# Feed-forward products of a streaming encoder step in two passes, one for each half of the frames

## The reference

```
for layer in range(2):
    x = rms_norm(h, g[0])
    m = mixer_ab(x) if layer == 0 else pool_mixer(x)
    h = h + rms_norm(m, g[1])
    x = rms_norm(h, g[2])
    gu = x @ ffn_w_in[layer]                               # 1024 x 5632
    y = (silu(gu[..., :2816]) * gu[..., 2816:]) @ ffn_w_out[layer]
    h = h + rms_norm(y, g[3])
```

## Time and profile before

| | us |
|---|---|
| median of 3 runs | 1102.53 |
| lowest, highest | 1100.94, 1103.25 |
| the profiled execution | 1102.74 |
| its span, first to last instruction | 1100.7 |
| PE busy in the span | 1063.5 |
| DVE busy | 506.5 |
| ACT busy | 363.5 |
| POOL busy | 43.7 |

### The profile page before, as it was taken

One profiled execution on the slowest core, in us unless ns is written; L12 is line 12 of the kernel. 1 busy time (PEld: TensorE's weight loads), 2 busy tenths in 40 slices (PEclk: granted clock), 3 DMA queues, 4 the chain that ended last, 5 costly groups with the idle time before them and its releaser, 6 DMA issues.

```text
span 1100.7 us, 19933 instructions
## 1 busy us (share of the span) xinstructions
PE 1063.5 (97%) x8219; PEld 1033.6 (94%) x8219; DVE 506.5 (46%) x813; ACT 363.5 (33%) x598; POOL 43.7 (4%) x48
## 2 busy tenths in 40 slices
PE   6999989989999999999999899899999999999997
PEld 4799789989999999999999799899999999999995
DVE  4386743855344444432222669544444443422225
ACT  5422344542222222222222665422222222222222
POOL 0070120000000000000000011000000000000000
PEclk9999999999999999999999999999999999999997
DMA  6422112213322332323323210232232232233212
GB/s 222 96 63 81 40 39 77 58 55 99 95 76 86 94 87 76 91 79 93 91 79 104 66 44 20 66 107 76 86 94 86 76 95 86 79 92 93 76 53 82
DMA packets 166532, 89.69 MB, mean 81 GB/s; under 512 B 11976, under 2 KB 163647, under 8 KB 166492
## 3 DMA queue, kind: packets, MB, share of 16 engines
q1 hardware_dynamic: 164620, 86.99, 27.0%
q10 hardware_dynamic: 1648, 1.78, 0.5%
q0 software_dynamic: 224, 0.35, 0.1%
HBM read 86.53 MB, written 2.58 MB: 81 GB/s over the span
## 4 chain that ended last, share of the span: by engine, by line
PE 85%; DVE 9%; ACT 2%; issue 2%; DMA 1%; SPq 0%; ACTq 0%; DVEq 0%
PE ps L453 27%; PE ps L454 27%; PE ps L455 27%; DVE h L1577 2%; DVE tmp L1547 1%; PE ps L518 1%; DVE acc_pre L1563 1%; DVE xlo L1551 1%; DVE wlo L1310 1%; DMA x_tok<-in_x_sample_dram 1%; PE ps L861 1%; ACT whi L936 0%; PE ps L471 0%; DVE va L1369 0%; PE ps L502 0%
## 5 line engine op out<-in xcount | busy, mean ns | idle before, releaser
L453 PE MATMUL ps<-xhi,whi 128*128 128x256 f32 (+1 forms) x1600 | 467.3, 292 | 13.7 <-DVE xlo L1551 5.8
L454 PE MATMUL ps<-xlo,whi 128*128 128x256 f32 (+1 forms) x1600 | 463.2, 289 | 0.0
L455 PE MATMUL ps<-xhi,wlo 128*128 128x256 f32 (+1 forms) x1600 | 462.0, 289 | 0.0
L453 PEld LDWEIGHTS ps<-xhi,whi 128*128 128x128 f32 x1600 | 304.3, 190 | 18.3 <-DVE xlo L1551 8.5
L1310 DVE TENSOR_TENSOR wlo<-raw,whi 128x1024 fp32r<-128x1024 f32 (+2 forms) x175 | 196.3, 1122 | 270.3 <-ACT whi L936 266.1
L455 PEld LDWEIGHTS ps<-xhi,wlo 128*128 128x128 f32 x1600 | 304.8, 190 | 0.0
L454 PEld LDWEIGHTS ps<-xlo,whi 128*128 128x128 f32 x1600 | 304.7, 190 | 0.0
L936 ACT ACTIVATE whi<-raw 128x1024 fp32r<-128x1024 f32 (+2 forms) x176 | 167.9, 954 | 197.3 <-PE ps L455 174.0
L455 PE MATMUL ps<-mhi,wlo 128*128 128x256 f32 (+1 forms) x704 | 203.5, 289 | 0.0
L453 PE MATMUL ps<-mhi,whi 128*128 128x256 f32 (+1 forms) x704 | 202.5, 288 | 0.0
L454 PE MATMUL ps<-mlo,whi 128*128 128x256 f32 (+1 forms) x704 | 202.4, 288 | 0.0
(11 more groups left out here) (194 smaller groups left out, 814.1 us busy)
## 6 DMA issues: line engine op xcount, KB each, us to landing
raw<-in_ffn_w_in_dram SPq DMA_DIRECT2D x88, 512.0 KB, 3.8
raw<-in_ffn_w_out_dram SPq DMA_DIRECT2D x32, 384.0 KB, 3.0
raw<-in_ffn_w_out_dram SPq DMA_DIRECT2D x32, 320.0 KB, 2.9
raw<-in_ab_w_in_dram SPq DMA_DIRECT2D x10, 512.0 KB, 3.8
x_tok<-in_x_prompt_dram SPq DMA_DIRECT2D x4, 512.0 KB, 5.2
raw<-in_ab_w_in_dram SPq DMA_DIRECT2D x8, 256.0 KB, 3.5
raw<-in_ab_w_out_dram SPq DMA_DIRECT2D x8, 256.0 KB, 2.8
raw<-in_ab_w_out_dram SPq DMA_DIRECT2D x16, 128.0 KB, 3.2
```

Of the source, the lines that this page charges most:

```text
L453: pe.matmul(out, wh, xh, start=first, stop=False)
L454: pe.matmul(out, wh, xl, start=False, stop=False)
L455: return pe.matmul(out, wl, xh, start=False, stop=last)
```

## The change

Each feed-forward product becomes two passes over its weights, one for half a and one for half b. A pass has 44 slots for gate and up or 32 for out, and in a slot PE uses one unit for one half, 24 matmuls (18 or 15 in out). The units are fetched and split again for the second pass, so 152 more units are transferred, and the ring raw has three places. The norms, residuals and the pooling layer of one half are cut into steps which every engine runs behind its own work of a slot; the table STAGE names the slot for (stage s, half b), with s = 0 for the mixer's residual, 1 for that of layer 0's feed-forward, 2 for the pooling layer's, 3 for the last. Half b of stage 0 stands in the gate-up pass of half a of layer 0, stages 1 and 2 of half a with the pooling in the out pass of half b, the same of half b in the gate-up pass of half a of layer 1, and stage 3 of half a in the last pass. In a step "sum" PE sums the squares of z and "pre" those of the new h; "scale" are four residual steps of two tiles each, "again" the second spread, "x" the four parts of the next x.

x is now multiplied by the gain and by r_pre before the product (`x_scale`, `x_high`, `x_low`), and the two multiplications behind it go. The gain of the post-norm is put into z by ACT. For half b within the passes root and inverse are one step on GpSimd, a power of -0.5 (`power`). The band matrices are no longer scaled by the norm; the rows are, when ACT copies them.

```diff
-NRAW, NSPLIT = 2, 4
+NRAW, NSPLIT = 3, 4
+C_AFTER = ((15, 17), (19, 21))
+STAGE = {
+    (0, 1): {"sum": 0, "spread": 2, "scale": (3, 5, 6, 8), "pre": 10, "again": 12, "x": (13, 15, 16, 18)},
...
+    (2, 0): {"sum": 21, "spread": 23, "scale": (24, 25, 26, 27), "pre": 29, "again": 31, "x": (32, 32, 33, 33)},
...
+    (2, 1): {"sum": 25, "spread": 27, "scale": (28, 30, 31, 33), "pre": 35, "again": 37, "x": (38, 40, 41, 43)},
...
+}
...
+def unit_sequence():
+    seq = [("in", j) for j in range(14)] + [("out", d) for d in range(KC)]
+    for layer in range(2):
+        for b in range(2):
+            for u in range(2 * FC):
+                seq.append(("gu", layer, b, u))
+                if layer and b == 0 and u in C_AFTER[1]:
+                    seq.append(("c", 1, C_AFTER[1].index(u)))
+        for b in range(2):
+            for n in range(4 * KC):
+                seq.append(("fo", layer, b, n))
+                if layer == 0 and b and n in C_AFTER[0]:
+                    seq.append(("c", 0, C_AFTER[0].index(n)))
+    return seq
...
@@ SP @@
-                        m = base + j
-                        sp.wait_ge(w_lo, i * 8 + (m - NRAW + 1))
-                        a, b = PIECES[j % 4]
-                        col = i * (2 * P) + (j // 4) * P
-                        sp.dma_start(tiles(m, (b - a) * P).rearrange("p (c n) -> p c n", n=P),
-                                     w_out[:, a:b, bass.ds(col, P)]).then_inc(w_loaded[m % NRAW], 16)
...
+            for m in range(U_OUT + KC, len(UNITS)):
+                if UNITS[m] == ("fo", 0, 1, 8):
+                    sp.wait_ge(w_used, FO_PASS[0, 0][-1] + 1)
...
+                load(m)
...
@@ PE @@
-                mm.then_inc(out_half_done if b == 0 else w_used, 1)
-                if e == 8:
-                    pe.wait_ge(acc_added, 8)
-                    sum_squares_half(1, 0)
-                if e == 9:
...
-                            pe.wait_ge(acc_added, Z_BEFORE[2 * layer + 1])
-                            pe.wait_ge(r_ready, spreads(n_post - 1))
-                            sum_squares_half(n_post, 1)
-                        if b == 0 and k == SPREAD_AT[layer]:
-                            spread_half(n_post, 1)
-                pe.wait_ge(pre_added, H_BEFORE[2 * layer + 1])
-                sum_squares(n_post + 1, acc_pre)
...
+            def sum_squares(s, b, pre):
+                if pre:
+                    pe.wait_ge(sq_added[b], 4 * s + 4)
+                else:
+                    pe.wait_ge(z_added[b], add_count(s, KC - 1))
+                    if s:
+                        pe.wait_ge(rstd_done[b], 2 * s)
+                short = pre and s == 1
+                for i, t in enumerate(POOL_ROWS[b]):
+                    t0, n = TILES[t]
+                    if not short:
+                        t0, n = t0 + n - P, P
+                    mm = pe.matmul(flat(6 + b, i, 1, n), acc[:, 0, t0:t0 + n], ones[:, :], start=True, stop=True)
+                mm.then_inc(sq_summed[b], 1)
+            def spread(s, b, pre):
+                pe.wait_ge(rstd_done[b], stat_count(s, pre))
+                if KEPT[s, pre] > 1:
+                    pe.wait_ge(r_kept[b], KEPT[s, pre] - 1)
+                for i, t in enumerate(POOL_ROWS[b]):
+                    w = TILES[t][1]
+                    lhs = rs[:, 3 * b + i:3 * b + i + 1].broadcast_to([P, P])
+                    mm = pe.matmul(flat(6 + b, P + i * P, w), lhs, ident[:, P - w:P], start=True, stop=True)
+                mm.then_inc(rstd_spread[b], 1)
...
+            def ffn_in(layer, b, run):
+                for slot, m in enumerate(GU_PASS[layer, b]):
+                    if UNITS[m][0] == "c":
+                        pool_products(m, 1)
+                        run(slot)
+                        continue
+                    f, j = divmod(UNITS[m][3], 2)
+                    i = inner(layer, b, f)
+                    pe.wait_ge(w_lo, m + 1)
...
+                        for p in range(KC // 2):
+                            pe.wait_ge(x_lo_done[b], 4 * layer + p + 1)
+                            mm = gate_up(m, bank, range(2 * p, 2 * p + 2), b)
+                            if p == KC // 2 - 1:
+                                mm.then_inc(w_used, 1)
+                            mm = gate_up(m + 1, bank + 1, range(2 * p, 2 * p + 2), b)
+                        mm.then_inc(w_used, 1)
+                    elif f or j == 0:
+                        gate_up(m, bank, range(KC), b).then_inc(w_used, 1)
+                    run(slot)
+                run(LAST)
...
+            def norms(s, b):
+                at = STAGE[s, b]
+                yield at["sum"]
+                sum_squares(s, b, 0)
+                yield at["spread"]
+                spread(s, b, 0)
+                if s == 3:
+                    return
+                yield at["pre"]
+                sum_squares(s, b, 1)
+                if s == 1:
+                    return
+                yield at["again"]
+                spread(s, b, 1)
...
@@ ACT @@
-                        act.wait_ge(gu_scaled, i * 2 + (FC * layer + f + 1))
-                        act.activation(tmp2[:, 0, :], tmp[:, 0, :], ACT.Silu).then_inc(silu_done, 1)
-                        hi_part(following + 2 * f, i2, step2)
-                        act.wait_ge(m_ready, i * 2 + (FC * layer + f + 1))
-                        act.activation(mhi[:, bass.ds(i * 2 + f, 1), :].rearrange("p o n -> p (o n)"), tmp2[:, 1, :],
-                                       ACT.Copy).then_inc(m_hi, 1)
-                        hi_part(following + 2 * f + 1, i2, step2)
...
+            def square_pair(s, b, p):
+                act.wait_ge(h_added[b], 4 * s + p + 1)
+                c = frames(b)
+                if p == 0:
+                    act.activation(acc[:, :, c], h[:, 0:2, c], ACT.Square).then_inc(h_squared[b], 1)
+                    return
+                if p >= 2:
+                    act.wait_ge(sq_added[b], 4 * s + p - 1)
+                act.activation(tmp2[:, :, c], h[:, 2 * p:2 * p + 2, c], ACT.Square).then_inc(h_squared[b], 1)
...
+                    f, j = divmod(UNITS[m][3], 2)
+                    i = inner(layer, b, f)
+                    bank = 2 * (f % 2) + j
+                    if j == 0:
+                        act.wait_ge(w_used, m + 1)
+                        if i >= 2:
+                            act.wait_ge(up_mult, i - 1)
+                        act.activation(tmp[:, f % 2, c], flat(bank, 0, n), ACT.Silu).then_inc(silu_done, 1)
+                        hi_part(m + 4)
+                    else:
+                        hi_part(m + 4)
+                        act.wait_ge(up_mult, i + 1)
+                        act.activation(mhi[b][:, f, :], tmp2[:, f % 2, c], ACT.Copy).then_inc(m_hi, 1)
+                    run(slot)
+                run(LAST)
...
@@ DVE @@
-                        dve.tensor_tensor(tmp[:, 0, :], gate, r, ALU.mult)
-                        dve.tensor_tensor(tmp[:, 1, :], up, r, ALU.mult).then_inc(gu_scaled, 1)
-                        lo_part(following + 2 * f, i2, step2)
-                        dve.wait_ge(silu_done, at(1))
-                        dve.tensor_tensor(tmp2[:, 1, :], tmp2[:, 0, :], tmp[:, 1, :], ALU.mult).then_inc(m_ready, 1)
-                        dve.wait_ge(m_hi, at(1))
-                        c = bass.ds(i * 2 + f, 1)
-                        dve.tensor_tensor(mlo[:, c, :].rearrange("p o n -> p (o n)"), tmp2[:, 1, :],
-                                          mhi[:, c, :].rearrange("p o n -> p (o n)").bitcast(F32), ALU.subtract)\
-                            .then_inc(m_lo, 1)
...
+            def fold_squares(s, b):
+                dve.wait_ge(sq_added[b], 4 * s + 3)
+                c = frames(b)
+                dve.tensor_tensor(acc[:, 0, c], acc[:, 0, c], acc[:, 1, c], ALU.add).then_inc(sq_added[b], 1)
+            def residual_pair(s, b, p):
+                c = frames(b)
+                src = (z_a, z_b)[b][:, 2 * p:2 * p + 2, :] if s == 2 else z[:, 2 * p:2 * p + 2, c]
+                if p:
+                    dve.wait_ge(h_added[b], 4 * s + p)
+                dve.tensor_tensor(tmp[:, :, c], src, pair_of(r_post, b), ALU.mult).then_inc(z_scaled[b], 1)
+                if p >= 2 and s < 3:
+                    add_square(s, b, p - 1)
+                dve.wait_ge(z_scaled[b], 4 * s + p + 1)
+                dve.tensor_tensor(h[:, 2 * p:2 * p + 2, c], h[:, 2 * p:2 * p + 2, c], tmp[:, :, c], ALU.add)\
+                    .then_inc(h_added[b], 1)
...
+            def x_scale(layer, b, p):
+                c = frames(b)
+                x = (tmp, tmp2)[p % 2]
+                if p >= 2:
+                    dve.wait_ge(x_lo_done[b], 4 * layer + p - 1)
+                for k in range(2):
+                    op = dve.scalar_tensor_tensor(x[:, k, c], h[:, 2 * p + k, c], gain(layer, 2, 2 * p + k),
+                                                  r_pre[:, c], ALU.mult, ALU.mult)
```

(36 more changed lines are left out.)

1295 lines of the change are left out of this document (653 added, 642 removed).

## The result

The changed kernel takes **1145.98 us** (1145.04 to 1147.09, 4 runs) against 1102.89 (1100.94 to 1103.63, 4 runs) before: 1.0403 times the time, 95% interval 1.0388 to 1.0418 (the two medians alone give 1.0391). Forecast were 1143.5 us, 3.7% slower. The profiled execution has a span of 1142.7 us where the sum gave 1141.7.

A forecast was written before the change was run, and what follows sets the result against it. PE was taken as the bound, busy 97% of the span. 202.1 + 16.4 + 792 + 52.3 + 48.7 + 9.0 + 21.2 gave a span of 1141.7, plus 1.8 outside it 1143.5 us, 3.7% slower; range 1110 to 1165.

The forecast's parts named there:

- tail: After the last feed-forward product: half b's residual, 24 transposes, copy and store, 21.2 us, one more than before.
- The five waits: PE's second sums of squares wait for DVE's last additions at five places: 8.3, 7.5, 9.0, 8.3, 8.8, together 41.9 us.
- bare: Least wait at such a sum from the order within its slot: 4.0 us gate-up, 2.9 product-out, 17.8 in all.
- backlog: Residual pairs make ACT and DVE take turns and run late ahead of the sums, raising waits to 41.9 us; chance 0.68.
- The first product: Transition into the first layer: first feed-forward product starts at 218.5, 16.4 us after the output products.
- The products: Both feed-forward layers: 6336 matmuls at 0.125 us on average, 792 us that neither kernel can avoid.
- The transposes: In the passes 40 transposes at 0.28 us, rounded to 11.5, and 16 of the last residual's half a, 4.5.
- The clock: After PE stands, its matmuls run at the lower clock: 1.5 us at each of six places, 9.0 us.
- The power step: GpSimd's replacement of root and inverse for half b: between 0.2 and 2.1 us, taken as costing nothing.
- The supply: Doubled weight transfers cost nothing; rival: 512 KB units one after another bind, 1280 us, chance 0.07 shared with slow power step.
- No backlog: Rival: ACT and DVE don't block each other at the five sums, so 17.8 replaces 41.9: 1119 us, chance 0.15.
- The halves hide all: Rival: no wait at the five sums, span 1083 without any wait, time 1087 us, faster than before; chance 0.10.

The follow-up runs named there:

- the kernel without the waits: Changed kernel with additions and sums of squares in separate slots everywhere, in the second set of slots (rows turned later, more room for bands and x parts): 1089.46 us, 0.9880.
- the run with three places: Changed kernel with three of PE's five second sums of squares treated in three ways (both moved later, only sum later, only additions earlier): 1138.22 us, 1.0317.

## Why the prediction was right

Term by term, from the starts in PE's timeline (all 6432 products with 256 or 288 columns; "products" are the 6336 of the feed-forward layers):

| us | forecast | measured |
|---|---|---|
| first feed-forward product | 218.5 | 217.4 |
| products at full clock | 792 | 798.0 |
| pooling products | 12.0 | 12.3 |
| turned rows and last transposes of half a | 16.0 | 6.4 |
| bands | 12.1 | 14.2 |
| norms' sums and spreads | 12.2 | 12.7 |
| waits of PE in the passes | 48.7 | 47.2 |
| lower clock, products in the stretches behind waits | 9.0 | 13.0 |
| spread over all other products | - | 4.0 |
| tail | 21.2 | 17.3 |
| span | 1141.7 | 1142.7 |

- **The five waits**, on which the verdict hung, were forecast as 8.3, 7.5, 9.0, 8.3 and 8.8 us and are 8.20, 7.39, 8.92, 8.29 and 8.69. What was reckoned from the order of the queues and the durations of the earlier trace rows held to a fiftieth there (for the parts of x it gave 5.3 against 4.6), and the runs show both halves of it: 3.84 bare, the rest backlog, and 1.14 with another order in the same slot.
- **The first product** was right to 1.1 us, with a wrong start: half a's residual begins at 196.23 and not at 198.4. From there to the end of the fold it takes 15.5 us (forecast 15.0), from the fold to the first product 5.7 (5.1).
- **The products** are 6 us dearer than 0.125 each. Half a starts 419 in 50 us and half b 377: 3168 x (50/419 + 50/377) = 798. The row of 802 in 100 us is of alternating halves; a pass of one half alone is a little slower on average. Why was not tried; nor was it for the 4.0 us spread over the products, of which the kernel without the waits still has 3.
- **The transposes** were priced by the wrong row. The 16 rows at 619.54 are products with `gain_diag`, two rows each; the changed kernel turns without the gain, and a transpose is a single row, 8 of them here in what adds 0.9 us between the products:

```profile
598.68 1.04 PE L909 MATMUL ps<-ident,h 128*128 128x128 f32 x8
```

  They start 0.11 us apart, where the forecast had 0.28. (The 0.28 was too dear even for a product of two rows: 2.21 us also hold three slower starts and the last row's way to its end, and otherwise the 16 rows start 0.11 apart, 0.22 for a product.) The Trainium skill (Perfetto Trace Analysis, Transposes) asks for the transpose instruction in place of a product with the identity where something is only turned, since it skips the arithmetic. The rows agree as to the time: 0.11 for a transpose, 0.22 for a filled product of the same shape. The same price makes most of the tail's 3.9 us: its 24 transposes, for which 8.8 us were reckoned, take 6.0 with the wait between them, nearly all at the lower clock, 0.21 apart.
- **The clock** cost 13 us and not 9. I took 1.5 us for each wait from the stretch behind one of 2.45 us. Behind the five, the products lose 1.4, 1.0, 2.5, 2.6 and 2.6 us, behind the x parts 2.2, behind the first product 0.7. The sums in such a stretch are slower too (1.44 us at 258.97; at the full clock 0.83), which is in the line of the norms. That products, clock and rest are 14 us over, and transposes and tail 13.5 under, is luck, and so is a span right to 1.0 us; the waits are not. The median lies 2.5 us above the forecast: 1.0 of the span, 0.5 more outside it (2.3 against 1.8), and 0.9 because the profiled execution was the fastest of the four.
- **The power step** took 0.85 to 0.89 us for 128 x 3, between its bounds of 0.2 and 2.1, and nothing waited for it in the kernel after (in the run with three places, with the rows in the slot of the sum, they did):

```profile
226.21 0.89 POOL L1909 TENSOR_TENSOR rs<-ms,minus_half 128x3 f32<-128x3 f32 x1 [71.60 <-DVE ms L1637]
```

- **The supply** holds with three places and costs 71 us with two. By the Trainium skill's rule (DMA: Bandwidth & Descriptors, Rules for kernel authors) of at least 1 MiB in one DMA for full bandwidth, the forecast's rival had the 512 KB units bind, at 1280 us. The runs don't bear that rival out: the same 512 KB units are enough with three places, where 183 GB/s are asked for. They don't speak against the rule itself, since full bandwidth wasn't needed. With two places it is the hand-over that binds: landing 3.8 us and two splits 2.3, shared by two places, are 3.05 us for a unit that half a uses up in 2.86.
- **The rivals.** "No backlog" falls with 3.84 against 8.20. "The halves hide all" had 1083 for the span without any wait; the kernel whose slots remove most waits has 1083.9. That they agree is partly the same luck: there too the products are some 6 us dearer, the transposes and the tail some 13 cheaper, and 3.3 us of waits are left from the first product to the last; and this execution was one of the two quickest of five (1086.23, median 1089.46). What the runs do show is that the halves gain and that the table as changed spent it.
